# Turning the q and k heads on VectorE instead of TensorE, and handing four weight units of each group to GpSimd

## The chip, the core and the metric

The kernel runs on one core of a Trainium2 chip. The metric is the time of one execution in microseconds (us) of device time. Engines are named as the profile names them: PE is TensorE, PEld its weight load, DVE is VectorE, ACT is ScalarE, POOL is GpSimd, SP is the queue that issues the loads.

## The reference, cut to what matters

One decoder layer, SEQ = 256 tokens, D = 2048, 16 heads of 128. The change touches the attention part:

```python
hn = rms_norm(x, norm_mix)
q, k, v = jnp.split(hn @ w_in, 3, axis=-1)            # w_in is 2048 x 6144
q = rms_norm(split_heads(q, 16, 128), q_gain)
k = rms_norm(split_heads(k, 16, 128), k_gain)
q = q * 128 ** -0.5
z = q @ k.T                                          # per head, strictly causal
a = exp(log_sigmoid(z) + rest)                       # rest: reversed running sum of log_sigmoid(-z)
x = x + (a @ v) @ w_out
x = x + (silu(h1 @ w_gate) * (h1 @ w_up)) @ w_down   # h1 = rms_norm(x), D_FF = 5632
x = x + sigmoid(rms_norm(x) @ ple_w_gate) * (p @ ple_w_proj)
```

## The kernel before, in words

**Split products.** Every matrix product is made of three fp32r products: the high part of each side, and each high part with the other side's low part (`TERMS`). A weight *unit* is two blocks of 128 rows by 512 columns: SP loads it into `raw`, ACT copies it to `w_hi` (`hi`, L443), DVE subtracts to get `w_lo` (`lo`, L702), and PE multiplies with it (`products`, L1047): 12 matmuls of 128x512, 6 for each of the two token blocks (tb 0, then tb 1). `RING` = 4 slots hold units, so `hi` of unit n waits until PE has used unit n-4 (`unit_used`), and SP's load of unit n waits for `lo` of unit n-4.

**Stages.** Stage A makes q, k, v for 4 heads at a time: 4 groups of 24 units, 8 for q, 8 for k, 8 for v. Stage B multiplies by `w_o`, C by gate and up, D by down, E by the last gate. q accumulates in `acc[0]`, k in `acc[1]`, v in `acc[0]` again, and so does the next group's q. Each accumulator half must be emptied (`acc_free`) before PE starts on it again. v is emptied in two steps: ACT `v_hi` (L525), then DVE `v_lo` (L769), both at step u = 1 of the next group in their own program.

**Order.** Each engine's program is a plain list. Loops over u = 0..23 place work at numbered steps: "at u = 13 of DVE" is a place in DVE's program and no time; ACT and DVE run up to 3 units ahead of PE. In a loop body over groups (`Fori`), group g's products carry the attention work of group g-1 (`attend(u, g - 1, A_EVERY)`): for head h, PE does `scores` at u = 3h, `rest` at 3h+3, `weigh` at 3h+6; DVE masks at 3h+3 and makes `log_terms` there, `exponent` at 3h+6, `weights_lo` at 3h+7, `keep_o` at 3h+9. Within one u PE does scores, weigh, rest, and then the unit's products.

**q and k heads.** When q (or k) is complete, ACT squares it (`square_heads`), DVE sums each head (`sum_heads`, L745), POOL makes the inverse root and the scale (`head_norm`: 11 small instructions, L395 to L404), DVE scales the accumulator into `normed` (`norm_heads`, L753), and then PE turns `normed` in two rounds of 4 transposes (`turn(0, normed, ...)`, L1080, into the PSUM tile `T[0]`), each followed by an ACT copy (`qT_hi`, `kT_hi`, L515) and a DVE subtraction (`qT_lo`, `kT_lo`, L761). The rounds stand at u = 12, 14 (q) and 20, 22 (k) of PE; in group 0 the first at 13.

The lines that place PE's work in a group:

```python
if not first:
    attend(u, g - 1, A_EVERY)
for i in range(2):
    for m in range(2):
        if u == (i + 1) * DU + 4 + 2 * m + (first and i == 0 and m == 0):
            left(pe, i, (A_P0 + 2 * g, A_P1 + g)[i] + 1)
            turn(0, normed, 2 * m, (X_ROUNDS + 1) // 2 + 4 * g + 2 * i + m)
before = A_P1 + g if part == 1 else A_P0 + 2 * g + part // 2
```

## Time and profile before

| | |
|---|---|
| median of 3 runs | 1225.83 us (1225.28 to 1226.48) |
| the profiled execution's own time | 1226.86 us |
| its span in the trace | 1223.9 us |
| busy: PE, PEld | 1217.5 us (99%), 1011.1 us (83%) |
| busy: DVE, ACT, POOL | 818.2 us (67%), 588.2 us (48%), 73.1 us (6%) |
| DMA | 229.32 MB, mean 187 GB/s |
| granted TensorE clock | 0.999 of full speed |

An engine's busy share tells how much of the span it had an instruction in work; PE instructions overlap, so PE's rate is read from the distance between the starts of two matmuls. The waits are read from the idle time ahead of an instruction and what ended it.

### The profile page before, as it was taken

Reading aid. Unit: us, or ns where it says so; the run is one execution under the profiler, and the core shown is the slowest. Engines: PE = TensorE matmul, PEld = TensorE weight load, DVE = VectorE, ACT = ScalarE, POOL = GpSimd, SP = SyncE. Lnnn points to the kernel's source line nnn. Section 1 sums busy time; section 2 is a strip of 40 time slices with the busy share of each in tenths; the row PEclk is TensorE's granted clock in tenths of the full one; section 3 lists DMA queues with packets and bytes.
Section 4 is the critical chain, followed back from the end, with each engine's and each line's share of the span. In section 5 each row is a group of like instructions: output and inputs, shape, how many; then the busy total and the mean of one; then the engine's idle time right before and its main releaser. Section 6 shows DMA issues by size and latency. Waiting matters only on the chain.

```text
span 1223.9 us, 17011 instructions
## 1 busy us (share of the span) xinstructions
PE 1217.5 (99%) x5524; PEld 1011.1 (83%) x5524; DVE 818.2 (67%) x1039; ACT 588.2 (48%) x727; POOL 73.1 (6%) x126
## 2 busy tenths in 40 slices
PE   9999999999999999999999999999999999999998
PEld 7888888888888888888888888888888888888886
DVE  5667576675779865776776677577665666655555
ACT  6555465554645534444443444444444444444443
POOL 0411102011000300000000000000000000002000
PEclk9999999999999999999999999999999999999999
DMA  7655465555555666666666666666565656474674
GB/s 267 209 184 161 151 189 157 185 154 160 174 165 173 208 190 203 191 190 186 205 190 186 205 189 187 189 205 187 173 216 164 221 164 225 154 229 152 192 230 131
DMA packets 120004, 229.32 MB, mean 187 GB/s; under 512 B 7538, under 2 KB 8868, under 8 KB 119972
## 3 DMA queue, kind: packets, MB, share of 16 engines
q1 hardware_dynamic: 119940, 228.90, 60.5%
q8 instruction: 18, 0.29, 0.1%
q14 instruction: 14, 0.11, 0.0%
q10 hardware_dynamic: 32, 0.01, 0.0%
HBM read 226.78 MB, written 2.10 MB: 187 GB/s over the span
## 4 chain that ended last, share of the span: by engine, by line
PE 66%; DMA 1%; DVE 0%; issue 0%; ACT 0%; ACTq 0%; SPq 0%; DVEq 0%
PE acc L1047 66%; DMA raw<-in_ple_w_gate 1%; DVE w_lo L702 0%; PE T L1080 0%; DVE stage L1011 0%; DVE x L1014 0%; DVE side L903 0%; ACT w_hi L443 0%; ACT stage L677 0%; SPq L264 0%; ACTq L442 0%; ACTq L440 0%; ACTq L671 0%; ACTq L676 0%; ACTq L674 0%
## 5 line engine op out<-in xcount | busy, mean ns | idle before, releaser
L702 DVE TENSOR_TENSOR w_lo<-raw,w_hi 128x1024 fp32r<-128x1024 f32 (+1 forms) x445 | 524.2, 1185 | 293.3 <-ACT w_hi L443 289.6
L443 ACT ACTIVATE w_hi<-raw 128x1024 fp32r<-128x1024 f32 (+1 forms) x445 | 452.6, 1021 | 552.8 <-PE acc L1047 514.5
L1047 PE MATMUL acc<-w_hi,xT_hi 128*128 128x512 f32 x1204 | 472.8, 393 | 0.3
L1047 PE MATMUL acc<-w_hi,xT_lo 128*128 128x512 f32 x1204 | 469.6, 390 | 0.0
L1047 PE MATMUL acc<-w_lo,xT_hi 128*128 128x512 f32 x1204 | 469.2, 390 | 0.0
L1047 PEld LDWEIGHTS acc<-w_hi,xT_hi 128*128 128x128 f32 x1204 | 226.2, 188 | 48.0 <-issue 1.3
L1047 PEld LDWEIGHTS acc<-w_hi,xT_lo 128*128 128x128 f32 x1204 | 226.1, 188 | 47.5
L1047 PEld LDWEIGHTS acc<-w_lo,xT_hi 128*128 128x128 f32 x1204 | 226.3, 188 | 45.6
L1047 PE MATMUL acc<-w_hi,hT_hi 128*128 128x512 f32 x352 | 137.1, 390 | 0.0
L1047 PE MATMUL acc<-w_lo,hT_hi 128*128 128x512 f32 x352 | 137.1, 390 | 0.0
L1047 PE MATMUL acc<-w_hi,hT_lo 128*128 128x512 f32 x352 | 137.1, 390 | 0.0
L903 DVE STREAM_TRANSPOSE side<-stage 32x256 f32<-32x256 f32 x272 | 118.5, 436 | 4.6
L1047 PEld LDWEIGHTS acc<-w_lo,hT_hi 128*128 128x128 f32 x352 | 66.1, 188 | 13.8
L1047 PEld LDWEIGHTS acc<-w_hi,hT_hi 128*128 128x128 f32 x352 | 66.1, 188 | 13.7
L1047 PEld LDWEIGHTS acc<-w_hi,hT_lo 128*128 128x128 f32 x352 | 66.1, 188 | 13.5
L411 POOL COPY x<-stage 128x1024 f32<-128x1024 f32 (+1 forms) x8 | 11.4, 1421 | 810.5 <-DVE stage L888 810.5
L1047 PE MATMUL acc<-w_hi,oT_hi 128*128 128x512 f32 x128 | 50.6, 396 | 0.0
L1047 PE MATMUL acc<-w_hi,oT_lo 128*128 128x512 f32 x128 | 50.0, 391 | 0.0
L1047 PE MATMUL acc<-w_lo,oT_hi 128*128 128x512 f32 x128 | 49.9, 390 | 0.0
L956 DVE TENSOR_TENSOR stage<-stage,acc 128x512 f32<-128x512 f32 x22 | 15.1, 688 | 26.8 <-PE acc L1047 26.8
L1047 PEld LDWEIGHTS acc<-w_hi,oT_lo 128*128 128x128 f32 x128 | 24.0, 188 | 5.2
L1047 PEld LDWEIGHTS acc<-w_lo,oT_hi 128*128 128x128 f32 x128 | 24.1, 188 | 4.7
(133 smaller groups left out, 626.1 us busy)
## 6 DMA issues: line engine op xcount, KB each, us to landing
raw<-in_sb_w_in SPq DMA_DIRECT2D x93, 512.0 KB, 3.7
raw<-in_ffn_w_gate SPq DMA_DIRECT2D x88, 512.0 KB, 3.7
raw<-in_ffn_w_up SPq DMA_DIRECT2D x88, 512.0 KB, 4.0
raw<-in_ffn_w_down SPq DMA_DIRECT2D x80, 512.0 KB, 4.7
raw<-in_sb_w_out SPq DMA_DIRECT2D x32, 512.0 KB, 3.8
raw<-in_ple_w_gate SPq DMA_DIRECT2D x20, 512.0 KB, 5.6
raw<-in_ple_w_gate SPq DMA_DIRECT2D x24, 256.0 KB, 3.3
raw<-in_ffn_w_down SPq DMA_DIRECT2D x16, 256.0 KB, 3.1
```

Source lines behind the costliest of these rows:

```text
L411: pool.tensor_copy(x[:, :, bass.ts(t, NT)], stage[:, :, :]).then_inc(x_stored, 1)
L443: act.activation(w_parts[0][:, slot(u), 0:n, :], raw[:, slot(u), 0:n, :], ACT.Copy).then_inc(hi_ready, 1)
L702: dve.tensor_tensor(w_parts[1][:, slot(u), 0:n, :], raw[:, slot(u), 0:n, :], w_parts[0][:, slot(u), 0:n, :].bitcast(F32), ALU.subtract).th ...
L903: last = dve.transpose(side[b * Q:(b + 1) * Q, :, :].rearrange("p c (t s) -> p t c s", t=TB)[:, :, :, a * Q:(a + 1) * Q], stage[a * Q:(a + ...
L956: dve.tensor_tensor(stage[:, tb, :], stage[:, tb, :], acc[1][tb][:, :], ALU.mult).then_inc(acc_free[1][tb], 1)
L1047: last = pe.matmul(acc[pair][tb][:, :], parts[a][:, c, tb * P:(tb + 1) * P], w_parts[w][:, slot(u), i, :], start=(start and i == 0 and n = ...
```

## The change

1. **Turning.** PE no longer turns `normed`. DVE turns it with 32x32 block transposes from SBUF to SBUF: 16 instructions for q, spread over steps 13 to 18 (`turn_q`, into the new tile `q_side`), and 16 for k at steps 20 to 22 (`turn_k`, into `k_side`, which is the memory of `squares`). ACT then copies all four heads at once to `qT_hi` (u = 20) and `kT_hi` (u = 0 of the next group), and DVE subtracts once for `qT_lo` (u = 21) and once for `kT_lo` (`k_lo`, u = 1 of the next group, ahead of `keep_v`).
2. **Low parts.** `lo` of units 13, 15, 20, 22 of each group is made by POOL. PE and SP wait on a semaphore of its own for those.
3. **Norm.** POOL's `head_norm` is 6 instructions instead of 11. DVE makes the mean square (2 small instructions in `sum_heads`) and multiplies by `rstd` while it writes `normed` (one `scalar_tensor_tensor` of the same size in place of a `tensor_tensor`). k's `norm_heads` stands at u = 20 instead of 21.
4. **Attention.** Inside the groups attention stands one step later (`A_FROM` = 1): `scores` of head 0 at u = 1, after the products of unit 0. In stage B it stands where it was.
5. **Straight code.** Loops of DVE, ACT and POOL are written out; those of PE and SP stay loops.

```diff
@@ -104,6 +104,13 @@
     R_AT, W_AT = 3, 6
+    A_FROM = 1
+
+    POOL_UNITS = (13, 15, 20, 22)
+    PN = len(POOL_UNITS)
+
+    Q_NORM, Q_TURN, Q_UNITS, Q_HI, Q_LO = 13, 13, 6, 20, 21
+    K_NORM, K_TURN, K_UNITS, K_HI, K_LO = 20, 20, 3, 0, 1
     Q = 32
@@ -388,22 +414,10 @@
             def head_norm(n, scale, step, pair_before, tiles_before):
-                pool.wait_ge(head_ssq_ready, n + 1)
-                pool.wait_ge(rstd_ready, 1)
-                for tb in range(TB):
-                    part = slice(tb * HG, (tb + 1) * HG)
-                    pool.tensor_scalar(head_ms[:, part], head_ssq[:, part], rstd2[:, tb:tb + 1], 1.0 / HD,
-                                       ALU.mult, ALU.mult).then_inc(pool_step, 1)
-                pool.wait_ge(pool_step, step + 2)
+                pool.wait_ge(head_ms_ready, TB * (n + 1))
                 pool.tensor_scalar(head_ms[:, :], head_ms[:, :], EPS, 1.0, ALU.add, ALU.mult).then_inc(pool_step, 1)
-                inverse_root(head_r[:, :], head_ms[:, :], HALF_MS, step + 3)
-                pool.wait_ge(pool_step, step + 8)
                 left(pool, pair_before, tiles_before)
-                for tb in range(TB):
-                    part = slice(tb * HG, (tb + 1) * HG)
-                    last = pool.tensor_scalar(head_scale[:, part], head_r[:, part], rstd[:, tb:tb + 1], scale,
-                                              ALU.mult, ALU.mult)
-                    last.then_inc(pool_step if tb == 0 else head_scale_ready, 1)
+                inverse_root(head_r[:, :], head_ms[:, :], HALF_MS, step + 1, scale, head_r_ready)
             def store_x(t, pair, tiles):
@@ -412,17 +426,24 @@
             norm(0, 0)
-            def head_norms(g):
+            def lo(U, u):
+
+                pool.wait_ge(hi_ready, U + 1)
+                pool.tensor_tensor(w_parts[1][:, slot(u), :, :], raw[:, slot(u), :, :],
+                                   w_parts[0][:, slot(u), :, :].bitcast(F32), ALU.subtract).then_inc(pool_lo_ready, 1)
+
+            for g in range(GROUPS):
                 head_norm(2 * g, HD ** -0.5, NORM_STEPS + 2 * g * HEAD_STEPS, 1, A_P1 + g)
+                for u in POOL_UNITS[:2]:
+                    lo(A0 + g * AU + u, u)
                 head_norm(2 * g + 1, 1.0, NORM_STEPS + (2 * g + 1) * HEAD_STEPS, 0, A_P0 + 2 * g + 1)
-
-            for g in range(GROUPS):
-                head_norms(g)
+                for u in POOL_UNITS[2:]:
+                    lo(A0 + g * AU + u, u)
             heads_end = NORM_STEPS + 2 * GROUPS * HEAD_STEPS
...
             norm(1, heads_end)
-            with nc.Fori(0, XN, engines=[mybir.EngineType.Pool], hint_back_edge=True) as t:
+            for t in range(0, XN):
                 store_x(t, 0, D_P0 + t + 1)
@@ -576,26 +597,28 @@
                     if not first:
+                        if u == K_HI:
+                            k_hi(g - 1)
                         if u == 1:
                             keep_v(g - 1, U0 - 1)
-                        attend(u, g - 1, A_EVERY)
-                    for part, (to, gain) in enumerate(((qT, QG), (kT, KG))):
+                        attend(u - A_FROM, g - 1, A_EVERY)
+                    for part in range(2):
                         end = (part + 1) * DU - 1
...
                             square_heads(U0 + end, 3 * g + part, 2 * g + part, part)
-                        if u == end + 8:
-                            turn_heads(to, gain, 4 * g + 2 * part, 0)
-
-                        if u == min(end + 10, AU - 1):
-                            turn_heads(to, gain, 4 * g + 2 * part + 1, 1)
+                    if u == Q_HI:
+                        act.wait_ge(q_side_ready, g + 1)
+                        act.activation(qT[0][:, :, :], q_side[:, :, :], ACT.Copy, scale=gains[:, QG:QG + 1]).then_inc(q_hi_ready, 1)
             group(0, first=True)
-            with nc.Fori(1, GROUPS, engines=[mybir.EngineType.Activation], hint_back_edge=True) as g:
+            for g in range(1, GROUPS):
                 group(g)
...
                 hi(B0 + u, u, len(blocks))
+                if u == K_HI:
+                    k_hi(GROUPS - 1)
                 if u == 1:
@@ -741,26 +764,59 @@
                 dve.wait_ge(squares_ready, n + 1)
-                dve.wait_ge(head_scale_ready, n)
+                dve.wait_ge(head_r_ready, n)
                 dve.reduce_sum(head_ssq[:, :], squares[:, :, :].rearrange("p t (h d) -> p (t h) d", d=HD),
                                AX_X).then_inc(head_ssq_ready, 1)
-
-            def norm_heads(n, pair, rounds):
-                dve.wait_ge(head_scale_ready, n + 1)
-                dve.wait_ge(T_ready, X_ROUNDS + rounds)
+                dve.wait_ge(rstd_ready, 1)
+                dve.wait_ge(head_ssq_ready, n + 1)
                 for tb in range(TB):
-                    factor = head_scale[:, tb * HG:(tb + 1) * HG].unsqueeze(2).broadcast_to([P, HG, HD])
-                    dve.tensor_tensor(normed[:, tb, :].rearrange("p (h d) -> p h d", d=HD),
-                                      acc[pair][tb][:, :].rearrange("p (h d) -> p h d", d=HD),
-                                      factor, ALU.mult).then_inc(acc_free[pair][tb], 1)
-
-            def turn_heads(to, gain, r, pair_of_heads):
-
-                part = slice(2 * pair_of_heads, 2 * pair_of_heads + 2)
-                dve.wait_ge(turned_hi, X_ROUNDS + r + 1)
-                dve.scalar_tensor_tensor(out=to[1][:, part, :], in0=T[0][:, :, :], scalar=gains[:, gain:gain + 1],
-                                         in1=to[0][:, part, :].bitcast(F32), op0=ALU.mult,
-                                         op1=ALU.subtract).then_inc(T_free[0], 1)
+                    part = slice(tb * HG, (tb + 1) * HG)
+                    dve.tensor_scalar(head_ms[:, part], head_ssq[:, part], rstd2[:, tb:tb + 1], 1.0 / HD,
+                                      ALU.mult, ALU.mult).then_inc(head_ms_ready, 1)
+
+            def norm_heads(n, pair, q_turned, k_turned):
+                dve.wait_ge(head_r_ready, n + 1)
+                dve.wait_ge(q_side_ready, q_turned)
+                dve.wait_ge(k_side_ready, k_turned)
+                for tb in range(TB):
+                    root = head_r[:, tb * HG:(tb + 1) * HG].unsqueeze(2).broadcast_to([P, HG, HD])
+                    dve.scalar_tensor_tensor(out=normed[:, tb, :].rearrange("p (h d) -> p h d", d=HD),
+                                             in0=acc[pair][tb][:, :].rearrange("p (h d) -> p h d", d=HD),
+                                             scalar=rstd[:, tb:tb + 1], in1=root,
+                                             op0=ALU.mult, op1=ALU.mult).then_inc(acc_free[pair][tb], 1)
+
+            def turn_heads(to, a, b):
+
+                return dve.transpose(
+                    to[b * Q:(b + 1) * Q, :, :].rearrange("p h (t s) -> p t h s", t=TB)[:, :, :, a * Q:(a + 1) * Q],
+                    normed[a * Q:(a + 1) * Q, :, :].rearrange("p t (h d) -> p t h d", d=HD)[:, :, :, b * Q:(b + 1) * Q])
+
+            def turn_q(g, i):
+
+                if i == 0:
+                    left(dve, 0, A_P0 + 2 * g + 1)
+                    dve.wait_ge(qT_ready, g)
+                for a, b in QUADRANTS[i * QN * QN // Q_UNITS:(i + 1) * QN * QN // Q_UNITS]:
+                    last = turn_heads(q_side, a, b)
+                if i == Q_UNITS - 1:
+                    last.then_inc(q_side_ready, 1)
+
+            def turn_k(g, i):
+
+                if i == 0:
+                    left(dve, 1, A_P1 + g + 1)
+                    dve.wait_ge(kT_ready, g)
+                    dve.wait_ge(head_ssq_ready, 2 * g + 2)
+                for a, b in QUADRANTS[i * QN * QN // K_UNITS:(i + 1) * QN * QN // K_UNITS]:
+                    last = turn_heads(k_side, a, b)
+                if i == K_UNITS - 1:
+                    last.then_inc(k_side_ready, 1)
+
+            def k_lo(g):
+                dve.wait_ge(k_hi_ready, g + 1)
+                dve.scalar_tensor_tensor(out=kT[1][:, :, :], in0=k_side, scalar=gains[:, KG:KG + 1],
+                                         in1=kT[0][:, :, :].bitcast(F32), op0=ALU.mult,
+                                         op1=ALU.subtract).then_inc(kT_ready, 1)
             def keep_v(g):
@@ -834,10 +890,11 @@
                     if not first:
-                        mask_scores(u, g - 1, A_EVERY)
+                        mask_scores(u - A_FROM, g - 1, A_EVERY)
                     if first and u == DU + 2:
                         sum_heads(0)
-                    lo(U0 + u, u, 2)
+                    if u not in POOL_UNITS:
+                        lo(U0 + u, u, 2)
                     if first and u == DU + 1:
@@ -851,27 +908,33 @@
                     if not first:
+                        if u == K_LO:
+                            k_lo(g - 1)
                         if u == 1:
                             keep_v(g - 1)
-                        attend(u, g - 1, A_EVERY)
-                    for part, (to, gain) in enumerate(((qT, QG), (kT, KG))):
+                        attend(u - A_FROM, g - 1, A_EVERY)
+                    for part in range(2):
                         end = (part + 1) * DU - 1
...
                             sum_heads(2 * g + part)
-                        if u == end + 6:
-                            norm_heads(2 * g + part, part, 4 * g + 2 * part)
-                        if u == end + 8:
-                            turn_heads(to, gain, 4 * g + 2 * part, 0)
-
-                        if u == min(end + 10, AU - 1):
-                            turn_heads(to, gain, 4 * g + 2 * part + 1, 1)
+                        if u == (Q_NORM, K_NORM)[part]:
+                            norm_heads(2 * g + part, part, g + part, g)
+                    if Q_TURN <= u < Q_TURN + Q_UNITS:
+                        turn_q(g, u - Q_TURN)
+                    if u == Q_LO:
+                        dve.wait_ge(q_hi_ready, g + 1)
+                        dve.scalar_tensor_tensor(out=qT[1][:, :, :], in0=q_side[:, :, :], scalar=gains[:, QG:QG + 1],
+                                                 in1=qT[0][:, :, :].bitcast(F32), op0=ALU.mult,
+                                                 op1=ALU.subtract).then_inc(qT_ready, 1)
+                    if K_TURN <= u < K_TURN + K_UNITS:
+                        turn_k(g, u - K_TURN)
             dve.wait_ge(gains_turned, 1)
...
             group(0, first=True)
-            with nc.Fori(1, GROUPS, engines=[mybir.EngineType.DVE], hint_back_edge=True) as g:
+            for g in range(1, GROUPS):
                 group(g)
@@ -891,6 +954,8 @@
                 lo(B0 + u, u, len(blocks))
+                if u == K_LO:
+                    k_lo(GROUPS - 1)
                 if u == 1:
@@ -1159,17 +1226,12 @@
                     if not first:
-                        attend(u, g - 1, A_EVERY)
-                    for i in range(2):
-                        for m in range(2):
-                            if u == (i + 1) * DU + 4 + 2 * m + (first and i == 0 and m == 0):
-                                left(pe, i, (A_P0 + 2 * g, A_P1 + g)[i] + 1)
-                                turn(0, normed, 2 * m, (X_ROUNDS + 1) // 2 + 4 * g + 2 * i + m)
+                        attend(u - A_FROM, g - 1, A_EVERY)
                     before = A_P1 + g if part == 1 else A_P0 + 2 * g + part // 2
...
                     else:
-                        products(U0 + u, u, xT, D_UNITS[k], part % 2, k == 0, k == DU - 1, before)
+                        products(U0 + u, u, xT, D_UNITS[k], part % 2, k == 0, k == DU - 1, before, (g, u))
                     if first and u + 2 < X_ROUNDS:
```

PE, at the start of a group's loop body (acc is an accumulator, Z the scores' tile). Before:

```order
L1047 MATMUL acc<-w_hi,xT_lo 128x512
L1196 UNCONDITIONAL_BRANCH
L1196 BRANCH_PREFETCH_HINT
L1196 ISA
L1101 ISA
L1094 MATMUL Z<-qT_hi,kT_hi 128x256
L1094 MATMUL Z<-qT_lo,kT_hi 128x256
L1094 MATMUL Z<-qT_hi,kT_lo 128x256
L1094 MATMUL Z<-qT_hi,kT_hi 128x128
L1094 MATMUL Z<-qT_lo,kT_hi 128x128
L1094 MATMUL Z<-qT_hi,kT_lo 128x128
L1041 ISA
```

The same place in the changed kernel:

```order
L1114 MATMUL acc<-w_hi,xT_lo 128x512
L1258 UNCONDITIONAL_BRANCH
L1258 BRANCH_PREFETCH_HINT
L1258 ISA
L1111 REGISTER_ALU
L1114 MATMUL acc<-w_hi,xT_hi 128x512
L1114 MATMUL acc<-w_lo,xT_hi 128x512
```

The six score matmuls that stood between the last v product of one group and the first q product of the next now stand twelve products later.

DVE, from the sum of the k heads (step 18) to the end of the group, in the loop body of before:

```order
L745 TENSOR_REDUCE head_ssq<-squares 128x8
L701 REGISTER_ALU
L702 TENSOR_TENSOR w_lo<-raw,w_hi 128x1024
L701 REGISTER_ALU
L702 TENSOR_TENSOR w_lo<-raw,w_hi 128x1024
L701 REGISTER_ALU
L702 TENSOR_TENSOR w_lo<-raw,w_hi 128x1024
L753 TENSOR_TENSOR normed<-acc,head_scale 128x512 x2
```

and of the changed kernel, on to the first steps of the next group (squares is the memory that `k_side` names):

```order
L768 TENSOR_REDUCE head_ssq<-squares 128x8
L774 TENSOR_SCALAR head_ms<-head_ssq,rstd 128x4 x2
L790 STREAM_TRANSPOSE q_side<-normed 32x2x4x32 x3
L725 TENSOR_TENSOR w_lo<-raw,w_hi 128x1024
L867 TENSOR_TENSOR oT_lo<-T,oT_hi 128x256
L783 SCALAR_TENSOR_TENSOR normed<-acc,rstd,head_r 128x512 x2
L790 STREAM_TRANSPOSE squares<-normed 32x2x4x32 x5
L725 TENSOR_TENSOR w_lo<-raw,w_hi 128x1024
L926 SCALAR_TENSOR_TENSOR qT_lo<-q_side,gains,qT_hi 128x1024
L790 STREAM_TRANSPOSE squares<-normed 32x2x4x32 x11
L725 TENSOR_TENSOR w_lo<-raw,w_hi 128x1024 x3
L817 SCALAR_TENSOR_TENSOR kT_lo<-squares,gains,kT_hi 128x1024
```

The transposes stand where DVE used to go from one unit's low part to the next, two low parts are gone from this stretch, and `kT_lo` stands right ahead of the two `v_lo` of `keep_v`.

DVE, steps 13 and 14 of a group with attention, in the changed kernel (oT_lo is `keep_o`, weight<-weight,R is `exponent`, weight_lo is `weights_lo`):

```order
L851 TENSOR_TENSOR neg_lo<-neg_log_1m,neg_hi 128x384
L783 SCALAR_TENSOR_TENSOR normed<-acc,rstd,head_r 128x512 x2
L790 STREAM_TRANSPOSE q_side<-normed 32x2x4x32 x2
L725 TENSOR_TENSOR w_lo<-raw,w_hi 128x1024
L862 TENSOR_TENSOR weight_lo<-weight,weight_hi 128x384
L790 STREAM_TRANSPOSE q_side<-normed 32x2x4x32 x6
```

The scaling of the q heads and the first two transposes now stand between `log_terms` and the `weight_lo` for which PE's `weigh` of head 2 waits.

## Rows read from the trace of the kernel before

**Rows 1.** The chain that ended last, in order of time: start us, us, what.

```profile
407.03 718.10 PE acc L1047 x3168
```

**Rows 2.** Busy time per engine in the third group's stretch, with clock and DMA share.

```profile
229.42:304.56 75.14, 75.14 (x369) 63.49 (x368) 51.85 (x69) 41.86 (x58) 10.41 (x20) 1.00 0.54 169
```

**Rows 3.** Timeline of PE around one turning round: start us, us, engine, line, operation.

```profile
298.43 0.39 PE L1047 MATMUL acc<-w_hi,xT_lo 128*128 128x512 f32 x1
298.65 0.60 PE L1080 MATMUL T<-ident,normed 128*128 128x128 f32 x4
...
299.01 0.48 PE L1047 MATMUL acc<-w_hi,xT_hi 128*128 128x512 f32 x1
...
299.79 0.39 PE L1047 MATMUL acc<-w_hi,xT_hi 128*128 128x512 f32 x1
```

**Rows 4.** Groups by line and shape: busy us, mean ns of one, then idle before.

```profile
L702 DVE TENSOR_TENSOR w_lo<-raw,w_hi 128x1024 fp32r<-128x1024 f32 x405 | 496.7, 1233 | 255.6 <-ACT w_hi L443 252.4
L443 ACT ACTIVATE w_hi<-raw 128x1024 fp32r<-128x1024 f32 x405 | 427.3, 1059 | 490.5 <-PE acc L1047 452.1 <-DMA raw<-in_ffn_w_down 17.0 <-DMA raw<-in_ple_w_gate 10.9
L903 DVE STREAM_TRANSPOSE side<-stage 32x256 f32<-32x256 f32 x272 | 118.5, 436 | 4.6
L761 DVE SCALAR_TENSOR_TENSOR qT_lo<-T,gains,qT_hi 128x512 fp32r<-128x512 f32 x8 | 6.0, 746 | 1.0 <-ACT qT_hi L515 1.0
L914 DVE SCALAR_TENSOR_TENSOR xT_lo<-side,gains,xT_hi 128x256 fp32r<-128x256 f32 x12 | 5.0, 473 | 0.0
```

**Rows 5.** Timelines of ACT, DVE and PE where group 2 ends and 3 begins.

```profile
228.26 0.69 ACT L525 ACTIVATE v_hi<-acc,rstd 128x512 fp32r<-128x512 f32 x1 [1.53 <-PE acc L1047]
...
228.98 0.75 DVE L769 SCALAR_TENSOR_TENSOR v_lo<-acc,rstd,v_hi 128x512 fp32r<-128x512 f32 x1 [0.81 <-ACT v_hi L525]
...
229.42 0.28 PE L1094 MATMUL Z<-qT_hi,kT_hi 128*128 128x256 f32 x1
```

**Rows 6.** Timeline in stage E, where an accumulator is emptied late.

```profile
1194.24 0.39 PE L1047 MATMUL acc<-w_hi,pT_lo 128*128 128x512 f32 x1
1194.64 0.19 PEld L1047 LDWEIGHTS acc<-w_hi,xT_hi 128*128 128x128 f32 x1 [0.43 <-ACT stage L677]
...
1195.22 0.40 PE L1047 MATMUL acc<-w_hi,xT_lo 128*128 128x512 f32 x1
```

**Rows 7.** Timelines of POOL and DVE where both work at once.

```profile
352.22 1.04 POOL L411 COPY x<-stage 128x1024 f32<-128x1024 f32 x1 [61.99 <-DVE stage L888]
352.37 1.97 DVE L702 TENSOR_TENSOR w_lo<-raw,w_hi 128x1024 fp32r<-128x1024 f32 x1 [0.30 <-ACT w_hi L443]
...
407.83 3.70 POOL L384 TENSOR_SCALAR mean_sq<-mean_sq 128x2 f32<-128x2 f32 x1
...
408.00 3.48 DVE L702 TENSOR_TENSOR w_lo<-raw,w_hi 128x1024 fp32r<-128x1024 f32 x3
...
941.26 1.79 POOL L411 COPY x<-stage 128x1024 f32 x1 [525.50 <-DVE stage L888]
...
942.07 1.32 DVE L903 STREAM_TRANSPOSE side<-stage 32x256 f32<-32x256 f32 x3
```

**Rows 8.** Timelines of ACT, DVE and POOL: the k heads of group 3.

```profile
282.04 0.60 ACT L510 ACTIVATE squares<-acc 128x512 f32<-128x512 f32 x1 [0.79 <-PE acc L1047]
...
282.67 1.22 DVE L745 TENSOR_REDUCE head_ssq<-squares 128x8 f32<-128x1024 f32 x1 [1.37 <-ACT squares L510]
...
285.48 0.20 POOL L398 TENSOR_SCALAR head_ms<-head_ms 128x8 f32<-128x8 f32 x1
...
288.33 0.20 POOL L372 TENSOR_TENSOR head_r<-head_r,newton 128x8 f32<-128x8 f32 x1
```

**Rows 9.** Timelines of PE and DVE: scores of head 3, then head 2 weighed.

```profile
257.90 0.28 PE L1094 MATMUL Z<-qT_hi,kT_hi 128*128 128x256 f32 x1
...
262.78 0.56 DVE L795 TENSOR_TENSOR neg_lo<-neg_log_1m,neg_hi 128x384 fp32r<-128x384 f32 x1
...
268.05 0.28 PE L1094 MATMUL T<-weight_hi,v_hi 128*128 128x256 f32 x1
```

76 lines of the change are left out of this document (48 added, 28 removed).

## Prediction, made before the changed kernel was run

> **What bounds the kernel now.** I read the table's busy shares first: PE 99%, DVE 67%. A busy PE proves little, so next comes the chain that ended last: from 407 us on it is one unbroken run of 3168 matmuls in 718.10 us [rows 1], 0.2267 us each, so a unit of 12 takes 2.72 us. PE waits for nobody there. In a group with attention it is the same: the third takes 75.14 us, PE busy throughout, DVE busy 51.85, POOL 10.41, at full clock and with DMA at 0.54 [rows 2]. PE's own instruction list sets the time; any instruction taken off PE is a gain, and other engines matter only where they come too late for PE.
>
> **What is removed.** Around a turning round, the last matmul before it starts at 298.43 and the fourth after it at 299.79 [rows 3]. Undisturbed it would start 4 x 0.2267 = 0.91 us later, at 299.34. A round costs PE 0.45 us. There are 16 (two for q and two for k in each of 4 groups): **-7.2 us**.
>
> The Trainium skill (VectorE: DVE Perf Modes, Rules for kernel authors) says to transpose 128x128 on TensorE if PSUM is a fine destination, and keep VectorE for 32x32 blocks. By engine time it has a point: DVE pays 16 x 0.44 = 7.1 us for what costs PE 0.9 us. It would decide here if DVE were the bound; by rows 2 it is not, so the rule's price is covered unless DVE falls behind somewhere.
>
> **What is added to DVE.** Durations [rows 4]: a low part 1.23 us (the next instruction can start about 1.15 after it), a block transpose 0.44 (same 256 elements per partition as in `side<-stage`), a `scalar_tensor_tensor` of 512 elements 0.75; from 256 elements at 0.47 and 512 at 0.75 I estimate 1.3 for the new `qT_lo` and `kT_lo` of 1024. Per group: +32 x 0.44 = 14.1, -4 x 1.2 = -4.8, two big subtractions for four small -0.4, scaling and the small mean squares about +0.7. DVE goes from 51.85 to about 61.5 of 73.5 us, 84%. It fits on average; the question is place.
>
> **The group boundary (new wait).** In the old trace the first half of v is emptied by ACT from 228.26 to 228.95 and by DVE from 228.98 to 229.73; PE finishes v's last matmuls and goes on at 229.42 with scores [rows 5]. Those six matmuls hid that `acc[0]` was still 0.31 us from free. Now unit 0 follows at once and waits. What a late release costs is in stage E: the weight load waits until 1194.64 for ACT, and the third matmul after the previous one at 1194.24 starts at 1195.22 instead of 1194.92 [rows 6], 0.58 after the load. Here the load can start at about 229.78, the third matmul at 230.36 instead of 229.42 + 0.45 = 229.87: 0.5 us. The second half is free about when PE comes for it. Three boundaries (0 to 1, 1 to 2, 2 to 3): **+1.5 us**. Stage B keeps its scores at step 0, so the fourth boundary keeps its cover, if `kT_lo` is ready.
>
> **The k heads' path to the boundary**, walked on group 3's clock. The squares end at 282.64, the sum runs 282.67 to 283.89 [rows 8]. New, from there: two small instructions of DVE (no row; the bounds are nothing and POOL's 0.2 each for the smallest instruction in rows 8; I take 0.4 for both) 284.3; POOL's six, 285.48 to 288.53 then, 3.05 us [rows 8], to 287.35 (before, the scaling began after 290); scaling 1.45, to 288.8; 5 transposes 291.0; low part of unit 21 292.2; `qT_lo` 293.5; 11 transposes 298.3; ACT's copy of k runs beside the low part of 23, done 299.5; units 24 and 25 (0 and 1 of the next) 301.8; `kT_lo` 303.1. PE's next group started at 304.56; now it does at 304.56 - 0.9 (two rounds) + 0.64 (`weigh` of head 3, now at step 16) = 304.3. So `v_hi` ends 0.47 before it [rows 5], at 303.8, and DVE has been free for 0.7 us. Low part 23 is needed at 301.6, done 299.5. In group 0, without attention, the start is 303.65 and the slack 0.1. So the boundary costs what rows 5 and 6 say, but only just: whatever makes DVE later than this by more than 0.7 us is paid in full, four times.
>
> **Step 13 and 14.** Scores of head 3 start at 257.90, `neg_lo` runs from 262.78 and the next can start at 263.25, PE weighs head 2 at 268.05 [rows 9]. Now scaling (1.4), two transposes (0.9), low part 14 (1.15) stand before `weight_lo` (0.55): 263.25, 264.65, 265.55, 266.7, 267.25, against a weight load at 267.8. It holds with 0.5 us to spare; before it held with over 2.
>
> **POOL's low part** has no row. A one-input copy of this size takes 1.04 us undisturbed [rows 7]; with two inputs I take twice that, 2.1. Bounds: 1.04, and twice the disturbed 1.8, 3.6. PE needs unit 13 over 8 us after POOL can begin; units 20 and 22 have 4 us or more; no value in the bounds makes a unit late by itself. The Trainium skill (GPSIMD Engine Reference, 3.1 Elementwise) has 4497 ns for 2048 elements, by which 1024 would take about 2.3 (an estimate from that page), and the sum would stay.
>
> **The shared port.** In rows 7 a POOL copy starts at 352.22 and ends at 353.26; the DVE low part that starts at 352.37 takes 1.97 instead of 1.23: it stood still until POOL had ended. The other way round, a tiny POOL instruction takes 3.70 us while three low parts run back to back, so a DVE in its stride keeps the port. Transposes at 942.07 take 0.44 each beside a POOL copy: they are not held. By my walk POOL's four units run beside transposes: 13 before `neg_lo`, 15 after `weight_lo` of head 2, 20 until 289.5 (low part 21 at 291.0), 22 after `qT_lo`, 293.5 to 295.6. Cost 0 when so.
>
> The Trainium skill (SBUF — State Buffer, Who interferes with whom) calls this an exclusive lock for the whole instruction; the trace agrees (1.97 against 1.23).
>
> **Loops, ACT, SP.** ACT makes 8 copies of 1024 elements in place of 16 of 512 and is busy 41.86 of 75.14 us [rows 2]. Loads of units 24 and 26 now wait for POOL, done about 6 us and more before ACT wants them. Loop branches stood on engines with slack. I cost these at 0, hidden by PE.
>
> **Sum.** 1226.86 - 7.2 + 1.5 = 1221.2 for a profiled execution; this one stands 1.03 above the median, so against the median 1225.83 - 5.7 = **1220.1 us**.
>
> **Rivals.**
> - *DVE is late at the boundaries and at `weigh`* (0.22). For: slacks of 0.7, 0.1 and 0.5 us rest on estimates of new shapes. Against: nothing in the walk exceeds them. If DVE is 1 us later than walked, 4 boundaries cost some 0.5 more and three weighs 0.5: +3.5, 1223.6; at 1.5 us 1226.
> - *The port goes to GpSimd first* (0.12), the slower side. Place: step 14. POOL's unit 15 can begin when ACT has its high part, at about 266.65; low part 14 starts at 265.55. If DVE is over 1.1 us later than walked there, POOL is first, low part 14 stands still for 2.1 and `weight_lo` comes 3.2 us late, 2.7 us after PE wants it, in three groups: +8; 1228. With POOL's unit at 4.5 us or more the gain would go too, since lows 16 and 21 would be held 1 us or more in each group. If POOL only slips in between low part 14 and `weight_lo` it is 1.6 x 3 = 5, about 1225.
> - *No boundary wait* (0.08): the release is taken up without loss, 1218.6. Rows 6 speak against it.
> - *The turning gives less than it seems* (0.08): the transposes' 0.45 is partly covered by something that PE then waits for anyway. For: ACT's and DVE's places are all new. PE's list without gaps speaks against it. Time 1223 to 1226.
> - The forecast itself: 0.50, its own range 1219.0 to 1222.3.
>
> **How the numbers follow.** Below 1217.8 I see no mechanism (all 16 rounds and nothing lost is 1218.6, 0.8 for error). Above, the late cases are taken in to 1226.3; port first, above it, is left out. A measurement tells 0.2%, 2.45 us, from no change: faster is under 1223.4. There lie the forecast, no wait, and 0.13 of the late and partial cases: 0.71. Within: 0.17 of them. Slower: 0.12.
>
> **What would show it.** Group starts of PE 73.9 us apart (75.14 - 1.8 + 0.5); PEld waits for DVE `v_lo` at three of them, near 0.5 us or less each; DVE transposes of 0.44; POOL's low part near 2.1 and DVE's at 1.23 with none near 3; PE's `weigh` without idle time. Wrong would be: gaps of PE over 1 us at `weigh` of head 2 or at the boundary, a gap ahead of the scores at stage B's start, or DVE low parts stretched beside POOL's.

## The result, and the profile after

The changed kernel takes **1238.59 us** (median of 6 runs, 1237.56 to 1243.84) against 1226.45 (6 runs) before: a ratio of 1.0109 [1.0087, 1.0132], 1.1% slower. The prediction had 1220.1 us (1217.8 to 1226.3) and gave "slower" a chance of 0.12. It was wrong in sign and size. The six single times lie in two bunches, 1237.56 to 1239.09 (four) and 1243.43 to 1243.84 (two); the profiled execution is the slowest of all, 1243.84 us (span 1241.9).

The chain that ended last, in order of time (start us, us, what), is no longer one run of matmuls:

```profile
419.80 713.12 PE acc L1114 x3146
1132.92 3.02 issue
1135.94 6.78 PE acc L1114 x22
```

Between them stands "issue": the engine waited for nothing that the profile shows. In [rows 1] the chain ran through this place. The groups by line and shape (busy us, mean ns of one, then idle before):

```profile
L725 DVE TENSOR_TENSOR w_lo<-raw,w_hi 128x1024 fp32r<-128x1024 f32 x389 | 479.0, 1239 | 235.4 <-ACT w_hi L464 231.4
L790 DVE STREAM_TRANSPOSE squares<-normed 32x256 f32<-32x256 f32 x64 | 27.9, 436 | 1.3
L432 POOL TENSOR_TENSOR w_lo<-raw,w_hi 128x1024 fp32r<-128x1024 f32 x16 | 41.4, 2590 | 24.0 <-ACT w_hi L464 23.7
L926 DVE SCALAR_TENSOR_TENSOR qT_lo<-q_side,gains,qT_hi 128x1024 fp32r<-128x1024 f32 x4 | 11.6, 2888 | 0.0
```

The transposes cost what [rows 4] said (0.44 us), and GpSimd's low part is 2.59 where 2.1 was taken. The fourth line is the odd one: `qT_lo` averages 2.89 us where 1.3 was estimated (1.27 in group 0, 3.43 in each of the other three).

Two kinds of idle time on TensorE are new. The first is a few waits for VectorE in every group. The timeline of PE at unit 23 of group 0 and where groups 0 and 1 meet (in brackets the idle time before, and who ended it):

```profile
75.52 0.39 PE L1114 MATMUL acc<-w_hi,xT_lo 128*128 128x512 f32 x1
77.22 0.50 PE L1114 MATMUL acc<-w_hi,xT_hi 128*128 128x512 f32 x1 [1.31 <-DVE w_lo L725]
...
79.86 0.39 PE L1114 MATMUL acc<-w_hi,xT_lo 128*128 128x512 f32 x1
81.34 0.50 PE L1114 MATMUL acc<-w_hi,xT_hi 128*128 128x512 f32 x1 [1.09 <-DVE v_lo L825]
```

From start to start these are 1.70 and 1.48 us where 0.23 is the pace. In groups 1 to 3 the gap at unit 23 is 1.14 each, at the other two boundaries 1.50 each, and ahead of stage B's scores there is one of 0.89 (the profile puts it down to "issue", but `kT_lo`, which the scores need, ended at 307.91, 0.11 before they started). Together 1.70 + 1.48 + 3 x 1.14 + 2 x 1.50 + 0.89 - 8 x 0.23 = **8.6 us**, where 1.5 was predicted.

The second kind waits for no engine. Timeline of PE at stage B's first product and at the third product of stage E:

```profile
308.62 0.27 PE L1161 MATMUL Z<-qT_hi,kT_lo 128*128 128x128 f32 x1
315.67 0.76 PE L1114 MATMUL acc<-w_hi,oT_hi 128*128 128x512 f32 x1 [6.77 <-issue]
316.23 0.63 PE L1114 MATMUL acc<-w_lo,oT_hi 128*128 128x512 f32 x1
...
1132.54 0.39 PE L1114 MATMUL acc<-w_lo,xT_hi 128*128 128x512 f32 x1
1135.94 0.40 PE L1114 MATMUL acc<-w_hi,xT_lo 128*128 128x512 f32 x1 [3.02 <-issue]
```

The windows of the idle time and of the stretch behind it (columns as in [rows 2]; PEclk is third from the end):

```profile
308.62:315.67 7.05, 0.28 (x4) 0.17 (x3) 5.14 (x8) 3.05 (x5) 0.00 (x0) 0.65 0.79 259
315.67:325.00 9.33, 9.33 (x33) 7.59 (x34) 1.66 (x2) 2.11 (x3) 0.00 (x0) 0.72 0.06 17
```

Behind the idle time the granted clock is at its lower level (1.2 in place of 2.4 GHz; 0.50 in window 315.67 to 320.92): 12 matmuls in that window go at 0.44 us each, which costs 2.5 us more. Behind the second stall nine such cost 1.6. So both stalls take 6.9 + 2.5 + 3.2 + 1.6 = **14.2 us** in this execution (each gap less the pace); what they take in the faster bunch was not profiled. In each of them lies one packet of q8. That is the queue that brings TensorE its instructions: over a whole execution it carries 18 packets in the kernel before, still 18 when the loops of the other engines are written out, and 43 when TensorE's are (the run `e13_pe_straight` below). The DMA view's queues in windows 308 to 312.5, 312.5 to 315.7 and 1132.9 to 1135.9:

```profile
q1 hardware_dynamic: 615, 1.19, 77.7%
...
q1 hardware_dynamic: 401, 0.76, 77.3%
q8 instruction: 1, 0.02, 1.8%
...
q1 hardware_dynamic: 50, 0.10, 9.4%
q8 instruction: 1, 0.02, 2.0%
```

The packet starts some 4.5 us into the first idle time. In the kernel before one had landed at 300 to 303 us, ahead of the need. A loaded DMA is not the reason: at the second stall q1's share is 9.4%. The Trainium skill (Runtime: NRT & Kernel Launch, Instruction fetch mechanics) says that instructions come in blocks of 256 and that a taken branch whose target has not been fetched forces a fetch. The trace agrees with the blocks (0.02 MB in each packet); the experiments show one thing more, that it matters where the loop's end lies in the block.

**Where VectorE loses its time.** Timelines of DVE, POOL and ACT at the end of group 3:

```profile
293.65 1.23 DVE L725 TENSOR_TENSOR w_lo<-raw,w_hi 128x1024 fp32r<-128x1024 f32 x1
294.80 3.43 DVE L926 SCALAR_TENSOR_TENSOR qT_lo<-q_side,gains,qT_hi 128x1024 fp32r<-128x1024 f32 x1
298.25 4.94 DVE L790 STREAM_TRANSPOSE squares<-normed 32x256 f32<-32x256 f32 x11
303.22 3.50 DVE L725 TENSOR_TENSOR w_lo<-raw,w_hi 128x1024 fp32r<-128x1024 f32 x3
306.63 1.28 DVE L817 SCALAR_TENSOR_TENSOR kT_lo<-squares,gains,kT_hi 128x1024 fp32r<-128x1024 f32 x1
307.83 1.41 DVE L825 SCALAR_TENSOR_TENSOR v_lo<-acc,rstd,v_hi 128x512 fp32r<-128x512 f32 x2
...
294.11 3.03 POOL L432 TENSOR_TENSOR w_lo<-raw,w_hi 128x1024 fp32r<-128x1024 f32 x1 [1.86 <-ACT w_hi L464]
...
306.20 0.69 ACT L546 ACTIVATE v_hi<-acc,rstd 128x512 fp32r<-128x512 f32 x1 [0.87 <-PE acc L1114]
```

POOL's unit 22 comes while low part 21 runs, ends 2.3 us behind it and so went ahead of `qT_lo`, which stood right behind on VectorE: 3.43 us in place of 1.27. (In group 0 it meets low part 21 itself, 3.19 us in place of 1.23.) Eleven transposes stand ahead of low part 23, for which PE waits, and three low parts and `kT_lo` ahead of v's low part, whose input was there at 306.89.

### The profile page after: what moved, and what is told of

Same layout as the page of the kernel before. It is cut to its first block, busy times and chain, and to the rows that moved or that the text cites. A ratio compares the mean times of both kernels' runs of the same rounds, so it can differ in the third digit from the quotient of the medians.

```text
span 1241.9 us, 15827 instructions
## 1 busy us (share of the span) xinstructions
PE 1217.4 (98%) x5460; PEld 1007.9 (81%) x5460; DVE 866.6 (70%) x1159; ACT 588.1 (47%) x719; POOL 96.7 (8%) x110
## 4 chain that ended last, share of the span: by engine, by line
PE 64%; DMA 1%; DVE 0%; issue 0%; ACT 0%; ACTq 0%; SPq 0%; DVEq 0%
PE acc L1114 64%; DMA raw<-in_ple_w_gate 1%; DVE w_lo L725 0%; PE T L1147 0%; DVE stage L1076 0%; ACT w_hi L464 0%; ACT stage L700 0%; DVE x L1079 0%; DVE side L968 0%; SPq L289 0%; ACTq L697 0%; ACTq L463 0%; DVEq L1073 0%
## 5 line engine op out<-in xcount | busy, mean ns | idle before, releaser
L725 DVE TENSOR_TENSOR w_lo<-raw,w_hi 128x1024 fp32r<-128x1024 f32 (+1 forms) x429 | 506.5, 1188 | 275.0 <-ACT w_hi L464 270.7
L425 POOL COPY x<-stage 128x1024 f32<-128x1024 f32 x8 | 11.8, 1472 | 816.1 <-DVE stage L951 816.1
L432 POOL TENSOR_TENSOR w_lo<-raw,w_hi 128x1024 fp32r<-128x1024 f32 x16 | 41.4, 2590 | 24.0 <-ACT w_hi L464 23.7
L1114 PEld LDWEIGHTS acc<-w_hi,oT_hi 128*128 128x128 f32 x128 | 24.7, 193 | 11.7 <-issue 6.9
```

The costliest lines, as they stand in the source:

```text
L425: pool.tensor_copy(x[:, :, bass.ts(t, NT)], stage[:, :, :]).then_inc(x_stored, 1)
L432: pool.tensor_tensor(w_parts[1][:, slot(u), :, :], raw[:, slot(u), :, :], w_parts[0][:, slot(u), :, :].bitcast(F32), ALU.subtract).then_in ...
L725: dve.tensor_tensor(w_parts[1][:, slot(u), 0:n, :], raw[:, slot(u), 0:n, :], w_parts[0][:, slot(u), 0:n, :].bitcast(F32), ALU.subtract).th ...
L1114: last = pe.matmul(acc[pair][tb][:, :], parts[a][:, c, tb * P:(tb + 1) * P], w_parts[w][:, slot(u), i, :], start=(start and i == 0 and n = ...
```

## The experiments

A ratio is this kernel over the kernel before, run on the same chip; the chips differ, and the kernel before took 1225.98 to 1226.74 us on them, so differences under 1 us between two runs are told by the ratios. The first six ask where the 14 us of the two stalls come from, the others where the 8.6 us of the groups do. "Gap" is from start to start of two matmuls.

**Padding, and the loops.** 80 increments of a semaphore that nobody reads go in front of matmuls of group 0. Some of them merge with what stood there; 74 instructions are left, and every loop of TensorE ends where it did before the change (the first at instruction 1520, a matmul counted as two; 1446 in the changed kernel).

```diff
+                            if pads[0] > 0:
+                                pads[0] -= 1
+                                pe.sem_inc(padding, 1)
```

> The changed kernel with 74 more instructions in PE's list in group 0 (80 semaphore increments, one ahead of each of 80 matmuls, some folded into others), so that PE's loops end where they end in the kernel before (instruction 1520 instead of 1446 for the first); nothing else differs. Theory L (PE runs out of fetched code behind a loop's end, since the end lies a few instructions ahead of a 256-instruction block boundary): the 6.8 us of PE idle at the start of stage B, the 3.0 us at the start of stage E and the half clock behind each go, about 9 to 13 us, 1238.6 to about 1228. Theory W (DVE or ACT are late there, the semaphores just do not show it): no change, 1238.6. Either way the gaps of 0.9 to 1.5 us at units 23 and 24 of each group stay.

Measured: 1227.51 us, 1.0012 [1.0003, 1.0022]. Both stalls are gone, the waits of the groups are all there. 74 instructions that do nothing take 11.1 us off the median. A block comes behind the loop's end here too (one q8 packet in window 309.5 to 312, where the first scores behind the loop start at 306.62), but TensorE still has instructions to go on with. Its PE timeline at the place of the 6.77 us:

```profile
307.22 0.28 PE L1166 MATMUL Z<-qT_hi,kT_lo 128*128 128x128 f32 x1
307.33 0.46 PE L1119 MATMUL acc<-w_hi,oT_hi 128*128 128x512 f32 x1
```

The reverse: the kernel before, padded by 182 instructions, so that its first loop ends at 1702, as far into a block as the changed kernel's 1446.

> The kernel before with 182 more instructions in PE's list in group 0, so that its loops end at the same places of a 256-instruction block as in the changed kernel (1702 and 1446 are both 166 beyond a multiple of 256). No other engine is touched. Theory L: the stalls at the start of stages B and E appear in the kernel before as well, with the lower clock behind them: 1226.4 + 9 to 13, about 1237. Theory W: 1226.4, or up to 1 us more for the added instructions.

Measured: 1231.92 us, 1.0055 [1.0037, 1.0073], where 1237 was expected; single times spread from 1228 to 1232 and from 1235 to 1236. The profiled one (1228.19 us, the fastest) has the stall in stage E only:

```profile
1119.75 0.39 PE L1052 MATMUL acc<-w_hi,xT_lo 128*128 128x512 f32 x1
1122.55 0.40 PE L1052 MATMUL acc<-w_hi,xT_hi 128*128 128x512 f32 x1 [2.41 <-issue]
```

So the layout can hurt the old kernel too, by half as much. Whether its slower executions have stage B's stall as well was not profiled. The kernel before with the loops of VectorE, ScalarE and GpSimd written out, and nothing else:

> The kernel before with only the loops of DVE, ACT and POOL written out; PE's list is the same. Theory L: no change, 1226.4 within 1.5 us. Theory F (the longer code of the other engines takes the fetches that PE needs): stalls of PE without a semaphore, 1230 or more.

Measured: 1225.69 us, 0.9997 [0.9987, 1.0006]. The straight code on those engines costs nothing. The changed kernel with TensorE's loops written out too:

```diff
-            with nc.Fori(1, GROUPS, engines=[mybir.EngineType.PE], hint_back_edge=True) as g:
+            for g in range(1, GROUPS):
```

> The changed kernel without padding, its four TensorE loops written out, so that TensorE never takes a branch back and its instructions come in one line. If the two stalls (6.8 us at stage B's start, 3.0 us at stage E) come of instruction blocks that are fetched only after a loop's end, they go, with the half clock behind them, and the time is that of the padded kernel, 1227 to 1228.5 us. If the fetch as such is what costs, there are now more than twice as many blocks and the time stays at 1238 or grows.

Measured: 1227.27 us, 1.0005 [0.9996, 1.0015]. With no branch back both stalls are gone, though far more instructions are fetched. The page's rows of the changed kernel's queue and of this one's (packets, MB, share):

```profile
q8 instruction: 17, 0.28, 0.1%
...
q8 instruction: 43, 0.70, 0.2%
```

It is not the fetching, but fetching behind a loop. Then two small paddings of the changed kernel, 8 and 29 instructions:

> The changed kernel with 8 more TensorE instructions. The stalled matmuls stood 17 and 6 instructions behind a loop's end, and the two places differ by a multiple of 256, which puts a block boundary at position 1455 to 1461 (and 4271 to 4277). With 8 more the first loop still ends ahead of its boundary (1454) and the third one behind it (4279). If a boundary shortly behind a loop's end makes the stall, the stall at stage B's start stays (4 to 7 us and the half clock) and the one in stage E goes: 1231 to 1236 us. If any shift takes both away, 1227.5; if it is no matter of position, 1238.

> The changed kernel with 29 more TensorE instructions: both loop ends (1475 and 4300) now lie behind the boundary, inside the next block. By the boundary theory both stalls go with less than half of the 74 instructions of the first padded run: 1227 to 1228.5 us. If it takes the whole shift of 74 (the places of before), one or both stay: 1231 to 1238 us.

Measured: 1235.32 us, 1.0073 [1.0056, 1.0090], with stage B's stall and, where stage E's had been, a gap of 0.85 us; and 1227.66 us, 1.0012 [1.0003, 1.0022], with neither. PE of the first:

```profile
306.91 0.28 PE L1166 MATMUL Z<-qT_hi,kT_lo 128*128 128x256 f32 x1
311.55 0.48 PE L1166 MATMUL Z<-qT_hi,kT_hi 128*128 128x128 f32 x1 [4.36 <-issue]
```

It comes three matmuls earlier than in the changed kernel: with the program pushed on by 8 instructions TensorE stops six sooner (three matmuls of two instructions), so at nearly the same address. The place is fixed in the program, and these runs fit that a loop must end shortly ahead of it.

**GpSimd's units.** The changed kernel with `POOL_UNITS = (13, 15, 20, 23)`:

> The changed kernel with unit 23 in place of unit 22 on POOL. Theory P (POOL's low part of unit 22 holds the port that DVE needs for qT_lo, 3.4 us instead of 1.3, or for the low part of unit 21 in group 0, and so k's turning, the low part of 23, kT_lo and v_lo come late): the PE gap at unit 23 goes, the one at the group boundary falls from 1.3 to about 0.5 us lost, in all about 7 us, 1238.6 to about 1231.5. Rival (DVE simply has too much in this stretch): the low part of 22 takes the place of the wait, under 2 us gained. The stall at stage B's start stays in both.

Measured: 1238.64 us, 1.0102 [1.0085, 1.0119]; the expected 1231.5 did not come. `qT_lo` takes 1.28 again and the gaps at unit 23 are gone, but low part 22, now VectorE's, took 1.97 beside GpSimd's unit 23, and the boundary gaps grew to 2.27: 7.5 us in the groups for 8.6. Both stalls stay, 4.98 and 3.25 us: stage B's is 2.1 us shorter than the changed kernel's. The padded kernel with `POOL_UNITS = ()`:

> The padded kernel with all 24 low parts of a group back on VectorE. That adds 4 x 1.23 us to VectorE's work of a group and takes GpSimd off the shared port. If GpSimd's grabs of the port are what made the waits (qT_lo 3.43 in place of 1.27, low part 21 3.19), these two go and the gaps at unit 23 (1.13 to 1.70 us) shrink, time at or below 1227.5 us. If the work that VectorE has between unit 20 and the boundary (normed heads, 16 transposes, six low parts, kT_lo, v_lo) is the cause, the gaps stay or grow by what 20 and 22 add (some 2.4 us a group less what the port gives back, 2.2), time 1227 to 1235 us.

Measured: 1228.66 us, 1.0019 [1.0010, 1.0029]. `qT_lo` takes 1.28 and yet the gaps stay (1.36 and three of about 1.2 at unit 23, 1.46 at the boundaries). Near unit 22 GpSimd costs VectorE 2.15 us at the port and spares it a low part of 1.15. In all the four units are worth some 1 us (1.0019 against 1.0012, and the two intervals overlap).

**Order at the boundary.** From here on all kernels are padded by the 74 instructions, if nothing else is said. First the scores back at unit 0 (`A_FROM = 0`):

> The padded kernel with the scores of the group before back at unit 0 as in the kernel before, so that they stand on TensorE ahead of the first product of the new tile. They need kT_lo, which lands at 307.9 us, as v's low part at 308.5 does just behind it. By the prediction's boundary term (the scores' matmuls as cover for v's emptying) the gap in front of the products goes but one in front of the scores takes its place: 1.5 falls to about 0.9 as at stage B, and the scores' own 1.3 us cover v: three times 0.6 us less, 1225 to 1226.5 us. If k's path is later than that there, the gap ahead of the scores is over 1.5 us and the time is 1227.5 or more.

Measured: 1227.89 us, 1.0013 [1.0004, 1.0023]. The boundary gap of 1.50 becomes one of 1.02 ahead of the scores, but unit 23's grows from 1.14 to 1.70: 8.9 us in the groups for 8.6. Giving back the cover, whose loss was the prediction's reason for a boundary wait, wins nothing.

```diff
-    K_NORM, K_TURN, K_UNITS, K_HI, K_LO = 20, 20, 3, 0, 1
+    K_NORM, K_TURN, K_UNITS, K_HI, K_LO = 20, 20, 4, 0, 1
```

> The padded kernel with k's 16 transposes over units 20 to 23 (four each) in place of 20 to 22 (5, 5, 6), so that low part 23 stands ahead of the last four. If VectorE's order makes the gap at unit 23, it falls from 1.13 to 1.70 us to about 0 in each group, since low part 23 comes 4 x 0.44 = 1.75 us earlier, while k's path ends as late as before or 1.2 us later (low part 23 now lies inside it): the boundary gaps stay at 1.5 us or grow towards 2.5. Time 1223.5 to 1227 us. If a wait elsewhere holds the units, gap 23 stays and the time is 1227.5.

Measured: 1238.67 us, 1.0094 [1.0073, 1.0115], a clear miss: the gaps at unit 23 go, but the boundary gaps grow to 4.38, 3.66 and 3.68 us, the one ahead of stage B's scores to 3.06, and behind each the granted clock is at 0.5 for some 3 us. PE and the windows at the first one, where 7 matmuls are at work in 2.82 us and the pace would give 12:

```profile
81.18 0.80 PE L1119 MATMUL acc<-w_hi,xT_hi 128*128 128x512 f32 x1 [4.00 <-DVE v_lo L826]
```

```profile
76.80:81.18 4.38, 0.39 (x2) 0.00 (x1) 3.48 (x5) 4.25 (x6) 0.00 (x0) 0.97 0.56 163
81.18:84.00 2.82, 2.82 (x7) 2.25 (x8) 2.82 (x3) 0.00 (x0) 0.00 (x0) 0.50 0.47 168
```

k's chain (transposes, ScalarE's copy, `kT_lo`) stands ahead of v on both engines, so its lateness is v's. With v first (`K_HI, K_LO = 2, 3`, `A_FROM = 2`):

> As the run with four transposes in each of units 20 to 23, and k's two parts made after v's (high part at unit 2, low part at unit 3 of the next group, first scores at unit 2), so that nothing of k stands ahead of the emptying of v's tile in the three group loops; in stage B k stays ahead of v. If k's path ahead of v on ScalarE and VectorE is what holds the boundary, the gaps of 1.50 us fall to what v's two halves take by themselves (some 1.0 us for the first) or less, in all 1222 to 1225 us, below the kernel before. If the boundary is v's emptying alone, they stay at 1.5 and the time is that of the run before.

Measured: 1227.78 us, 1.0014 [1.0003, 1.0025]. The boundary gaps are 2.15, 1.48 and 1.48, in place of 3.7 and more: k ahead of v made them grow. But they only come back to the padded kernel's 1.50, and 3.07 us are left ahead of stage B's scores, so the expected 1222 to 1225 did not come. Low parts 0 and 1 still stand ahead of v's. Next v behind unit 0, and the last group's turning over three units:

```diff
-                        if u == 1:
+                        if u == 0:
                             keep_v(g - 1)
```

> The run with v ahead of k, and two more steps: v's two parts stand behind the next group's unit 0 on ScalarE and VectorE in place of behind unit 1, and the last group turns k over three units again. The trace of that run shows low parts 0 and 1 on VectorE at 225.28 to 227.6 us while v's high part was there at 226.64, and v's low part only at 227.56. If VectorE's order is what holds the boundary, the three gaps of 1.48 us fall to 0.5 to 0.8, and the gap of 3.06 ahead of stage B's scores to 0.9 to 2.0 with 0 to 1.1 at unit 23 there: time 1222 to 1225 us. If the boundary is held by v's emptying itself, the gaps stay and the time is 1226.5 to 1228.

Measured: 1226.16 us, 1.0001 [0.9991, 1.0010]. The boundary gaps are 1.05, 0.60 and 0.60, so low parts ahead of v's were the cause of the 1.50. But gaps of 1.31, 1.69 and 1.71 us come ahead of the scores, where `kT_lo` is late, and at the last group 1.15 at unit 23 and 0.88 ahead of the scores are left: 1222 to 1225 was expected. PE:

```profile
228.31 0.50 PE L1120 MATMUL acc<-w_hi,xT_hi 128*128 128x512 f32 x1 [0.21 <-DVE v_lo L827]
...
235.45 0.38 PE L1167 MATMUL Z<-qT_hi,kT_hi 128*128 128x256 f32 x1 [1.32 <-DVE kT_lo L819]
```

The same with the scores at unit 3, padded and with TensorE's loops written out:

> The run with v's parts behind unit 0, and the first scores at unit 3 in place of unit 2, so that kT_lo (behind unit 3 on VectorE) is there when TensorE comes to them. If VectorE's order is all that eats the gain, the three gaps of 1.3 to 1.7 us ahead of the scores go (4.1 us less the 0.23 each of the pace), and nothing takes their place: 1221.5 to 1222.8 us, faster than the kernel before by some 4 us. If something else holds the group, a gap comes up elsewhere and the time is 1225 to 1226.5.

> The same order without padding, TensorE's loops written out. By the block theory no loop's end is left at which a fetch could be late: 1221.3 to 1222.8 us, the same as the padded one within 0.5 us. If the padded one gains by its places alone, this one is slower by over 1 us.

Measured: 1226.86 us, 1.0009 [1.0000, 1.0018], and 1226.42 us, 1.0004 [0.9995, 1.0013]. The expected 1222 did not come. The gaps ahead of the scores are gone, and two of 0.9 per group stand ahead of `weigh`, whose `weight_lo` now stands on VectorE behind a sum, three transposes of q and a low part:

```profile
210.33 0.39 PE L1120 MATMUL acc<-w_hi,xT_lo 128*128 128x512 f32 x1
211.25 0.39 PE L1167 MATMUL T<-weight_hi,v_hi 128*128 128x256 f32 x1 [0.54 <-DVE weight_lo L864]
```

This order with other units on GpSimd, none and (13, 15, 22, 23):

> The padded kernel with scores at unit 3, all low parts on VectorE. If VectorE's load around the boundary has slack once v goes first, the time is that of the run with GpSimd's four within 0.7 us (1221.5 to 1223.5). If the four low parts are what lets VectorE keep up, gaps of 1 to 2 us come back at units 0, 1 or 23 of each group: 1224 to 1228 us.

> The padded kernel with scores at unit 3, GpSimd making units 13, 15, 22 and 23 in place of 13, 15, 20 and 22, so that no low part stands behind the 16 transposes of k on VectorE. If low part 23 on VectorE is what holds unit 23 of the last group (1.15 us), that gap goes and the one ahead of stage B's scores grows by as much less the low part's 1.2: 0 to 1.2 us less in all, 1220.5 to 1222.5. If low part 20, now on VectorE ahead of k's normed heads, puts k's path back by its 1.2 us, nothing is won: 1221.5 to 1223.5.

Measured: 1224.76 us, 0.9986 [0.9977, 0.9995], with one gap of 0.68 per group ahead of `weigh`; and 1233.01 us, 1.0060 [1.0044, 1.0075]. The second is a miss. VectorE's side of it:

```profile
292.92 3.22 DVE L726 TENSOR_TENSOR w_lo<-raw,w_hi 128x1024 fp32r<-128x1024 f32 x1
...
296.40 3.09 DVE L928 SCALAR_TENSOR_TENSOR qT_lo<-q_side,gains,qT_hi 128x1024 fp32r<-128x1024 f32 x1
```

Each stood still beside one of GpSimd's two units (292.67, 2.40 us, and 295.39, 3.02 us), and stage B's scores came after a gap of 4.51, with the granted clock at 0.5 behind it. Last, k one unit earlier (`K_HI, K_LO = 1, 2`) with the scores at unit 2, with GpSimd's four units and without:

> The run with v's parts behind unit 0 and scores at unit 2, with k's high part at unit 1 and its low part at unit 2 (in place of 2 and 3). From that run's trace kT_lo would start at about 232.2 instead of 233.89 us and be done at 233.4, before TensorE comes to the scores (233.97). If VectorE's order is the whole cause, the three gaps of 1.3 to 1.7 us go and the time is 1222 to 1223.5 us, faster than the kernel before by 2.5 to 4. If VectorE has no room left at units 13 to 18, gaps of 0.5 to 1.5 us come up at the weigh steps and the time is 1224.5 to 1226.5.

> As the run before it, all low parts on VectorE. With scores at unit 3 taking GpSimd's four away made it 2.1 us faster (1224.76 against 1226.86). If that is the shared port (qT_lo 3.43 in place of 1.27 us), this one is faster than the run before it by 0.5 to 2 us: 1220.5 to 1223. If it was only the weigh steps' place, VectorE's 4.9 us more per group make this one 0 to 2 us slower: 1223 to 1226.

Measured: **1223.29 us**, 0.9975 [0.9965, 0.9985], and 1223.99 us, 0.9977 [0.9967, 0.9986]. Both beat the two kernels of this study, the first by 3.4 us and 15.3 us. The two do not differ beyond their intervals; that the second would be 0.5 to 2 us faster, by the port, did not come true. The gaps at the boundaries are 1.03, 0.60, 0.60, ahead of the scores 0.77 and 0.72 in groups 2 and 3, and 1.15 at unit 23 and 0.88 ahead of the scores at the last one. The chain that ended last in the first:

```profile
289.39 3.34 DVE qT_lo L928
...
404.89 718.11 PE acc L1120 x3168
```

The 718 us of [rows 1] are whole again, and `qT_lo`, held by the port, is still a piece of the chain.

## Why the prediction was wrong

- *"Loops, ACT, SP ... I cost these at 0, hidden by PE"*: **the step that failed most, some 11 of the 12.1 us.** It is the same step as *"any instruction taken off PE is a gain"*: the instructions that leave PE were counted as time and never as places in its program. The loops of the other engines are harmless (0.9997); that PE's list is 74 shorter moves a loop's end to just ahead of a block's end, and PE waits for its own instructions. Shown by 8, 29 and 74 instructions of padding and by the written-out loops. No rival had it. (11.1 is the difference of the two medians, of different chips; each against the kernel before on its own chip, 12.1 and 1.4, it is 10.7.) Open stays what decides when the block is fetched: the old kernel with its first loop ending equally far into a block had no stall at stage B in the profiled execution, and with unit 23 on GpSimd the same stall lasted 4.98 us, not 7.05. Nor is it shown why the first stall lasts 7 us where the packet's own time is under 1 us.
- *"Three boundaries: +1.5 us"* from slacks of 0.7 us and, for unit 23, 2.1: mis-sized, it measured **8.6**. Walked on the new clock (k's squares end 1.98 us later, at 284.62) the eleven transposes should have ended at 300.3; they ended at 303.19, 2.9 late. Of this 2.15 is the port at `qT_lo`, the rest 0.4 to 0.6 in POOL's small chain, which took 3.45 and not 3.05, and in small hand-overs. Low part 23 then came 0.9 us too late (a gap of 1.14 for 0.23), and v's low part began 0.9 us after its input was there (307.83 and 306.89).
- *"A DVE in its stride keeps the port. ... Cost 0"*: failed. [Rows 7] show tiny POOL instructions beside three low parts; a POOL tensor operation that came while VectorE's ran went before VectorE's next. The rival "GpSimd first" had the mechanism, at step 14, where nothing happened; it happened at unit 22. The Trainium skill (SBUF — State Buffer, Who interferes with whom) calls the port a lock for one instruction at a time, and this trace agrees, 3.43 us against 1.27. But it is no more than a part: without GpSimd's units the gaps stay.
- *"DVE is late at the boundaries"* (0.22) was the rival that came true in the groups. It priced its 1 us of lateness at 0.5 per boundary; unit 23, which it didn't name, cost as much as the boundary.
- *"-7.2 us"* for the turning was right within about 1 us. The padded kernel, without the stalls, is 1.4 us slower than the kernel before (1227.51 against 1226.1), which is 8.6 - 7.2. In the two traces stage B's first product starts at 307.33 against 305.20, 2.1 us later. The group period, forecast at 73.9, is 75.8 (79.86, 155.60, 231.37).
- Right too: transposes 0.44, `kT_lo` 1.28, no idle time at `weigh`.

The order that gives 1223.29 us keeps k out of v's way; 1.03 + 2 x 0.60 + 0.77 + 0.72 + 1.15 + 0.88 - 7 x 0.23 = 4.1 us of gaps over the pace remain in its groups.

## What to carry to other kernels

When an edit adds or removes instructions on the engine that sets the time, compare first where its loops end in blocks of 256 instructions, and try the kernel once with some padding or with the loops written out before judging the edit. An average share of VectorE's busy time (84% forecast, 63.95 of 75.77 us measured) says nothing about a tile's end: write down who stands ahead of the instruction that frees the tile, on each engine, and put that first. A queue walked with slacks under 1 us needs the worst case of the shared port in it, 2.2 us each time that a GpSimd tensor operation can arrive while VectorE runs one.

## What was not expected of the hardware

- TensorE stood still for 7.05 us (6.77 of them "issue") and 3.40 us (3.02) within some 20 instructions behind a loop's end, with one packet of the instruction queue (0.02 MB) inside each; 29 dummy instructions, or no loop, removed both.
- The length of an idle gap of TensorE alone did not tell whether the granted clock fell to 0.5. It did at or soon behind all nine gaps of 3.25 to 7.05 us in these traces, and behind one of 3.06 us (four transposes a unit). It did not behind one of 3.07 us (v first), nor behind those of 2.15, 2.24 and 2.80 us. With unit 23 on GpSimd there were three gaps of 2.27 us: behind the first the clock was at 0.5 from 80.1 to 83.4 us, behind the other two it stayed at 1.00. Where it fell it cost up to 2.5 us beside the gap.
- A GpSimd `tensor_tensor` of 1024 elements took 2.40 us by itself and made VectorE's next two-input operation 3.1 to 3.4 us long in place of 1.23 to 1.28, though VectorE had instructions back to back.
